# State-space decays of a two-block kernel: the running sums made once with heads on partitions, and picked per head by 64-row matmuls

## The reference, cut to what matters

```python
x = (xh * dt[..., None]).reshape(Bsz, nc, CHUNK, SSD_GROUPS, R, P)
a_cs = jnp.cumsum((dt * A).reshape(Bsz, nc, CHUNK, SSD_GROUPS, R), axis=2)
seg = a_cs[:, :, :, None] - a_cs[:, :, None, :]
decay = jnp.exp(jnp.where(causal, seg, -jnp.inf))
cb = jnp.einsum('bclgn,bcsgn->bclsg', Cc, Bc)
y_diag = jnp.einsum('bclsg,bclsgr,bcsgrp->bclgrp', cb, decay, x)
```

## Time and profile before

| | us |
|---|---|
| median of 3 runs | 1393.29 (1392.86 to 1393.83) |
| the profiled execution's own time | 1393.55 |
| its span | 1391.7 |
| PE busy | 1331.1 (96%) |
| DVE busy | 944.4 (68%) |
| ACT busy | 766.4 (55%) |
| POOL busy | 206.7 (15%) |

### The profile page before, as it was taken

The page is one execution under the profiler, slowest core; times in us unless marked ns, Lnnn a source line. Parts: engine busy times, 40 slices in busy tenths (PEclk is TensorE's granted clock), DMA queues, the critical chain, the costliest instruction groups (busy, mean ns, idle before and its releaser), DMA issues.

```text
span 1391.7 us, 23083 instructions
## 1 busy us (share of the span) xinstructions
PE 1331.1 (96%) x9022; PEld 1211.4 (87%) x9022; DVE 944.4 (68%) x1369; ACT 766.4 (55%) x1150; POOL 206.7 (15%) x165
## 2 busy tenths in 40 slices
PE   9999999999898999999999998989999999999997
PEld 8999989888898999989998887889999788787876
DVE  6555575485466555556688774765665899999996
ACT  5333345665446333355564676325635577777774
POOL 1111120040001111120301322510001000202020
PEclk9999999999999999999999999989999999999999
DMA  9655544522345655544443343314454699999991
GB/s 312 209 188 182 181 140 158 194 79 90 127 140 161 202 181 184 181 133 152 152 164 125 126 137 99 92 56 157 143 195 152 225 393 369 337 369 336 369 330 53
DMA packets 73944, 263.44 MB, mean 189 GB/s; under 512 B 8321, under 2 KB 9601, under 8 KB 73729
## 3 DMA queue, kind: packets, MB, share of 16 engines
q1 hardware_dynamic: 72864, 260.39, 55.0%
q10 hardware_dynamic: 992, 1.86, 0.4%
HBM read 261.17 MB, written 1.05 MB: 188 GB/s over the span
## 4 chain that ended last, share of the span: by engine, by line
PE 62%; DVE 10%; ACT 6%; issue 2%; POOL 1%; DVEq 0%; ACTq 0%; POOLq 0%
PE bank L561 19%; PE bank L563 18%; PE bank L562 18%; DVE sb_wlo L518 3%; DVE sb_wlo L505 2%; PE bank L2777 1%; ACT sb_Uh L636 1%; ACT sb_aw L1726 1%; DVE sb_XC L2114 1%; ACT sb_whi L489 1%; PE bank L2834 1%; ACT sb_XC L1697 0%; PE bank L653 0%; POOL sb_Xe L2436 0%; ACT sb_XC L1759 0%
## 5 line engine op out<-in xcount | busy, mean ns | idle before, releaser
L505 DVE TENSOR_TENSOR sb_wlo<-sb_raw,sb_whi 128x1024 fp32r<-128x1024 f32 (+2 forms) x304 | 384.8, 1310 | 174.9 <-ACT sb_whi L489 174.7
L489 ACT ACTIVATE sb_whi<-sb_raw 128x1024 fp32r<-128x1024 f32 (+3 forms) x308 | 301.8, 1031 | 234.8 <-PE bank L563 228.6
L561 PE MATMUL bank<-sb_Uh,sb_whi 128*128 128x256 f32 x1216 | 348.4, 287 | 10.8 <-DVE sb_wlo L505 4.3
L562 PE MATMUL bank<-sb_Ul,sb_whi 128*128 128x256 f32 x1216 | 344.7, 283 | 0.0
L563 PE MATMUL bank<-sb_Uh,sb_wlo 128*128 128x256 f32 x1216 | 344.7, 283 | 0.0
L561 PEld LDWEIGHTS bank<-sb_Uh,sb_whi 128*128 128x128 f32 x1216 | 233.7, 192 | 15.7 <-issue 8.0
L562 PEld LDWEIGHTS bank<-sb_Ul,sb_whi 128*128 128x128 f32 x1216 | 233.9, 192 | 0.9
L563 PEld LDWEIGHTS bank<-sb_Uh,sb_wlo 128*128 128x128 f32 x1216 | 233.8, 192 | 0.0
L561 PE MATMUL bank<-sb_whi,sb_Uh 128*128 128x256 f32 (+3 forms) x560 | 162.4, 290 | 7.2 <-DVE sb_Ul L645 5.4
L562 PE MATMUL bank<-sb_wlo,sb_Uh 128*128 128x256 f32 (+3 forms) x560 | 159.8, 285 | 0.0
L563 PE MATMUL bank<-sb_whi,sb_Ul 128*128 128x256 f32 (+3 forms) x560 | 159.7, 285 | 0.0
(11 more groups left out here) (407 smaller groups left out, 2261.9 us busy)
## 6 DMA issues: line engine op xcount, KB each, us to landing
sb_raw<-in_slabs SPq DMA_DIRECT2D x162, 512.0 KB, 4.6
sb_raw<-in_ffn_in SPq DMA_DIRECT2D x88, 512.0 KB, 4.5
sb_raw<-in_moe_in SPq DMA_DIRECT2D x50, 512.0 KB, 5.5
sb_raw<-in_ffn_out SPq DMA_DIRECT2D x44, 512.0 KB, 4.0
sb_raw<-in_moe_out SPq DMA_DIRECT2D x26, 512.0 KB, 5.9
sb_deep_free<-in_moe_in SPq DMA_DIRECT2D x16, 512.0 KB, 5.6
sb_deep_uh<-in_moe_in SPq DMA_DIRECT2D x16, 512.0 KB, 5.3
sb_deep_ul<-in_moe_in SPq DMA_DIRECT2D x16, 512.0 KB, 5.8
```

The source lines that it names most:

```text
L489: nc.scalar.activation(whi[:, i % NSLOT, c], raw[:, i % NSLOT, c], ACT.Copy).then_inc(S("hi_done"), 1)
L505: nc.vector.tensor_tensor(wlo[:, i % NSLOT, c], raw[:, i % NSLOT, c], whi[:, i % NSLOT, c].bitcast(F32), ALU.subtract).then_inc(S("lo_done ...
L561: pe.matmul(o, lh, rh, start=start, stop=False, skip_group_check=True)
L562: pe.matmul(o, lh, rl, start=False, stop=False, skip_group_check=True)
```

## The change

A constant `pick` is added: 128 rows by 32 columns, with a one where row modulo 32 equals the column. DVE makes three things more:

- `DTR`, in the top-k rounds: `dt * A` repeated four times along the free dimension (128 x 256);
- `PICKR`: `pick` in the rounded format (float32r);
- `CST`: TensorE multiplies `DTR` by `upto` (two float32 matmuls, bank 4), which gives the running sums with heads on partitions, four copies of the 32 heads, tokens along the free dimension. DVE copies them out rounded, and writes in the second and the fourth group of 32 partitions what the rounding lost. Partitions 0 to 63 and 64 to 127 so each hold a high part and a low part of all heads.

The eight decay matmuls of a round then take 64 rows: the weights are a head's column of `PICKR`, read with a step of zero, the moving operand is the tile of `CST`, in float32r. The array sums high and low part, and every output row is the head's running sum as before. The first four heads of a round use rows 0 to 63, the other four rows 64 to 127, and the matmuls of the two halves alternate, into two banks, both claimed ahead of them.

```diff
+        ("pick", (np.arange(P)[:, None] % SH == np.arange(SH)[None, :]) * 1.0),
...
+            CST = sb("CST", [P, T], F32R, p2)
+            PICKR = sb("PICKR", [P, SH], F32R, p2)
+            DTR = sb("DTR", [P, NT, P // SH, SH], F32, p2)
...
+                    dve.wait_ge(*reach("dt_d", 2))
+                    dve.tensor_copy(DTR[:], ssm[:, 2:4].unsqueeze(2).to_broadcast([P, NT, P // SH, SH])).then_inc(S("dt_d"), 1)
...
+            dve.tensor_copy(PICKR[:], const("pick")).then_inc(S("cst"), 1)
+            dve.wait_ge(*reach("cst_mm", 1))
+            dve.tensor_copy(CST[:], bank[4][:, 0:T]).then_inc(S("cst"), 1)
+            dve.wait_ge(*reach("cst", 2))
+            for r in (SH, 3 * SH):
+                dve.tensor_tensor(CST[r:r + SH, :], bank[4][r:r + SH, 0:T], CST[r:r + SH, :].bitcast(F32), ALU.subtract).then_inc(S("cst"), 1)
...
-            pe.wait_ge(*reach("dt_d", 2))
+            pe.wait_ge(*reach("dt_d", 3))
...
+            claim(4, "cst", 4)
+            for t in range(NT):
+                last = pe.matmul(bank[4][:, t * P:(t + 1) * P], DTR[:, t].rearrange("p a h -> p (a h)"), const("upto"),
+                                 start=t == 0, stop=True, skip_group_check=True)
+            last.then_inc(S("cst_mm"), 1)
...
+                    if u == 0:
+                        pe.wait_ge(*reach("cst", 4))
                     for k in range(2):
-                        n = 2 * u + k
-                        claim(n % 4, "seg", n + 1)
-                        for h in range(4):
-                            col = ssm[:, 2 + t, 8 * g + 4 * k + h:8 * g + 4 * k + h + 1].to_broadcast([P, P])
-                            last = pe.matmul(bank[n % 4][:, h * P:(h + 1) * P], col, const("upto"), start=h == 0, stop=True,
-                                             skip_group_check=True)
-                        last.then_inc(S("seg_mm"), 1)
+                        claim((2 * u + k) % 4, "seg", 2 * u + k + 1)
+                    for h in range(4):
+                        for k in range(2):
+                            rows, hd = slice(64 * k, 64 * k + 64), 8 * g + 4 * k + h
+                            last = pe.matmul(bank[(2 * u + k) % 4][:, h * P:(h + 1) * P], PICKR[rows, hd:hd + 1].to_broadcast([64, P]),
+                                             CST[rows, t * P:(t + 1) * P], start=h == 0, stop=True, skip_group_check=True)
+                            if h == 3:
+                                last.then_inc(S("seg_mm"), 1)
```

## The result

The changed kernel takes 1396.67 us in the median of 19 runs (1393.63 to 1399.9), the kernel before 1393.1 (1388.92 to 1394.49, 19 runs): a ratio of 1.003 with a 95% interval of 1.0021 to 1.0038, some 4.2 us slower. The forecast was 1393.1 us and "no change", with a range of 1389.5 to 1395.6 us; the median lies above that range, and the outcome "slower by over 0.2%" had been given a chance of 0.10. The profiled execution took 1398.26 us, with a span of 1396.5 and a mean granted clock of 0.978; before it was 1393.55, 1391.7 and 0.983.

The account below looks back on a forecast made before the run. The prediction took TensorE, busy for 96% of the span, as the bound, except where it waits afterwards. Savings of 3.6 us, clock falls of 2.8 and 0.6 at the end summed to -0.2: 1393.1 us, range 1389.5 to 1395.6.

Parts of the forecast that it names:

- The round: One round of eight decay matmuls on TensorE: 0.64 us as four overlapping pairs, saving 1.13 us, bounds 0.69 to 1.33.
- Where it counts: State-space loop: rounds 1, 4 and 5 save 1.13 us each, round 6 0.2, rounds 0, 2, 3, 7 nothing; 3.6 us.
- The falls of the clock: Rounds 2 and 3: waits for Xe grow to about 2.6 us, clock falls to 1.2 GHz, 1.4 us each, 2.8 together.
- the end of the loop: Round 7: the clock can fall before L2772 rather than behind it, costing 0.6 us, up to 0.95.
- the clock holds: Rival for rounds 2 and 3: no fall behind the longer waits, full 3.6 us gain, 1389.7 us; chance 0.22.
- The rival of long falls: Rounds 2 and 3: low clock for 7 us, not 3.4, up to 3.2 us each, 1396.7 us; chance 0.11.
- The rest at nothing: Added float32 matmuls, DVE's copy to DTR, CST and PICKR instructions: hidden beside other work, costed at 0; last group 1.5 uncovered.
- The sum: Whole kernel: -3.6 + 2.8 + 0.6 = -0.2 us, giving 1393.1 us against the median of 1393.29.

Follow-up runs that it names:

- one_half_shift256: Changed kernel plus an unused 128-byte hole, the four upper-half heads all ahead of the four lower-half ones instead of alternating: 1395.7 us, ratio 1.0001 against the kernel before.
- after_shift256: Changed kernel plus an unused 128-byte hole behind the constants, so buffers lie 256 bytes later than in the kernel before: 1394.84 us, ratio 1.0009 against the kernel before.
- fill23: Changed kernel plus ten filler matmuls of zeros ahead of the wait for Xe in rounds 2 and 3: 1394.44 us, ratio 1.0011 against the kernel before.
- old_less_work: Kernel before with six of eight decay matmuls left out in rounds 2 and 3, nothing else changed: 1398.17 us, ratio 1.0028 against the kernel before.
- prep_only: Changed kernel with the decay matmuls of before; DTR, CST and PICKR made but not used: 1395.22 us, ratio 1.0019 against the kernel before.
- before_shift128: Kernel before plus an unused 128-byte buffer behind the constants, no other edit: 1396.21 us, ratio 1.0018 against the kernel before.

## Why the prediction was wrong, step by step

**The round: right.** The forecast was 0.64 us, with 1.13 saved, and in the rows it is 0.59 us to the next instruction in round 1. The four pairs, too, are in the trace (one_half_shift256, above). Where there is no wait, from outputs to outputs, before has 9.33 and 10.18 us in rounds 4 and 5, and after 8.28 and 9.13: 1.05 saved each time, within the bounds of 0.69 and 1.33.

**Where it counts: right, but for round 1 in this trace.** Rounds 2 and 3 gave nothing: the state matmul starts 872.19 - 868.77 = 3.42 us behind the first decay matmul, as before (3.51). Round 6 gave 0.13 (forecast 0.2). Round 1 gave nothing in the profiled execution, since of the slow stretch of round 0 5.4 us lay behind the state matmul and not 3.1. From that state matmul to the outputs in round 1 it is 16.39 us after and 16.27 before. In after_shift256 and fill23 3.0 us of the slow stretch lie behind it, though it lasted 6.8 us there too, and the way takes 15.24 and 15.35 us: there the 1.0 us are seen.

**The falls of the clock: right in mechanism, a little small.** Both came, behind 2.75 us of waiting (2.6 forecast). From outputs to outputs, rounds 2 and 3 took 13.36 and 13.38 us and not 11.77 and 11.78: 1.6 us more each, against the 1.4 forecast, 3.2 in place of 2.8. At the end of the loop 1.2 us were lost and not 0.6, in a slow stretch of 17.1 us. The rival "the clock holds" is out for rounds 2 and 3. The Trainium skill (TensorE: Matmul & The Clock Gate, "Why this matters for your kernels") warns of somewhat longer gaps only, by which the clock would have held; here it fell behind 2.75 and 2.84 us, and the measurement decides. The rival of long falls didn't come in rounds 2 and 3 of after; old_less_work shows that it can. That rival's sum was 1396.7 us, just what was measured, and this is luck: its mechanism isn't in the trace.

**The rest at nothing: this step failed.** The prediction asked of the added instructions only whether their time is hidden, and it is (the first state matmul at 850.56, before 850.60; prep_only has nothing left beyond what an empty hole costs). It didn't ask what the constant's 128 bytes do to the buffers behind it. This term, which the prediction put at 0 without a word, is 2.5 us (1.1 to 3.9, before_shift128): the largest error, and the one for which the range had no room. It was in no row of the stage that I read: it lies in the feed-forward stages.

**The sum, put right.** Clock and work alone gave -0.2 in the prediction. With three times 1.05 and 0.13 for round 6 (-3.3), 3.2 for the falls and 1.2 for the end it is +1.1, and after_shift256 measured +1.3 (-0.3 to 2.9). In the profiled execution of after, where round 1 gave nothing, it is +2.2, the 2.2 us by which it is behind at the end of the stage. With 2.5 for the moved buffers it is 3.6, and 4.2 were measured (2.9 to 5.3). The forecast lay 3.6 us below the median of the runs; 2.5 of them are the buffers', 1.0 are the falls and the end of the loop.

## What to carry to other kernels

Work taken away ahead of a wait can be worse than worth nothing. If the wait grows and the clock falls behind it, the saving costs time, and the same saving pays when other work is moved into the wait (here it lost some 1.3 us with the waits and gained 4.0 us in the stage, and 5.7 by the ratios, without most of them). Compare, before you believe a small difference, the pace of the instructions that the change doesn't touch, from start to start; a new constant or buffer moves all that is made behind it, and an unused hole of the same size in the old kernel tells its price. A single profiled execution has chance in it (here 2 to 3 us, by where the clock falls), so a cause is settled by ratios of several runs and not by two traces.

## What was not expected of the hardware

- The pace of matmuls went with the place of the buffers in the SBUF. With all buffers behind the constants where they were, 128 bytes further and 256 bytes further in each partition, the float32r matmuls of 512 columns on hh and hl were 227.9, 232.3 and 227.9 ns apart in the feed-forward stages. Only these three places were tried, and only by moving the whole set of buffers, so neither the rule nor which of the moved buffers matters is settled.
- Two decay matmuls in place of eight, in two rounds, made a kernel slower by 0.28% (old_less_work), since the clock fell to 1.2 GHz behind waits of 2.84 us.
- In 64-row form, eight matmuls of 128 columns take 0.59 us when the halves alternate and 0.60 when they come one after the other. In both orders they start in pairs, one of each half, a few ns apart.
